# A two-layer transformer kernel: who copies the down weights of lanes 1 and 2 in the second mixture of experts

## The reference, cut to what matters

```python
N_EXPERTS_2 = 64; TOP_K_2 = 8; D_EXPERT = 256
...
    _, eidx = lax.top_k(jnp.where(emask, sel, -jnp.inf), TOP_K_2)
...
    def block_ffn(args):
        xb, e = args
        return (jax.nn.silu(xb @ w_gate[e]) * (xb @ w_up[e])) @ w_down[e]

    yb = lax.map(block_ffn, (xin, blk_e)).reshape(NB * MOE_BLOCK, D)
    y_assign = yb[dest] * sw[:, None].astype(yb.dtype)
    routed = jax.ops.segment_sum(y_assign, stok, num_segments=T)
```

## Time and profile before

| | before |
|---|---|
| runs | 3305.33, 3311.96 and 3310.26 us, median 3310.26 us |
| the profiled execution, its own time | 3302.2 us |
| its span | 3299.9 us |
| mean granted clock of TensorE | 0.952 |
| PE busy in the span | 2963.0 us, 90% |
| DVE busy | 1822.8 us, 55% |
| ACT busy | 1202.7 us, 36% |
| POOL busy | 824.5 us, 25% |

### The profile page before, as it was taken

One profiled execution on the slowest core, in us unless ns is written; L12 is line 12 of the kernel. 1 busy time (PEld: TensorE's weight loads), 2 busy tenths in 40 slices (PEclk: granted clock), 3 DMA queues, 4 the chain that ended last, 5 costly groups with the idle time before them and its releaser, 6 DMA issues. The chain is left out here.

```text
span 3299.9 us, 53016 instructions
## 1 busy us (share of the span) xinstructions
PE 2963.0 (90%) x17159; PEld 1407.0 (43%) x17160; DVE 1822.8 (55%) x2799; ACT 1202.7 (36%) x1768; POOL 824.5 (25%) x918
## 2 busy tenths in 40 slices
PE   8999989996999999498959999898889999999992
PEld 4444445553666445232326777344423322222230
DVE  3221234445777312444435777334478887888885
ACT  2222133333545100111113333021157766666774
POOL 1100000000000000144541000000058766767772
PEclk9999999997999999699978999898989999999996
DMA  6221021114122220589952000213179999999996
GB/s 242 85 107 44 0 90 51 51 50 101 52 63 67 71 72 32 221 355 417 416 216 90 26 25 29 89 49 109 67 293 317 340 377 379 316 356 350 342 303 198
DMA packets 188557, 565.56 MB, mean 171 GB/s; under 512 B 25468, under 2 KB 103904, under 8 KB 151296
## 3 DMA queue, kind: packets, MB, share of 16 engines
q1 hardware_dynamic: 146576, 425.10, 34.0%
q0 software_dynamic: 36912, 126.39, 13.2%
q10 hardware_dynamic: 4968, 12.74, 1.0%
HBM read 463.30 MB, written 100.86 MB: 171 GB/s over the span
## 5 line engine op out<-in xcount | busy, mean ns | idle before, releaser
L1561 POOL COPY moe_idx<-moe_slot_idx 128x4 int32<-128x4 int32 x4 | 0.6, 188 | 1804.3 <-DVE moe_slot_idx L1739 1804.3
L1466 POOL DMA_INDIRECT moe_xb<-token_rows,moe_idx x408 | 421.5, 1033 | 108.9 <-issue 95.0
L2135 DVE COPY h<-w_gu 128x1024 f32 (+1 forms) x342 | 266.2, 779 | 235.6 <-PE gu_ps L2003 153.7
L2029 PE MATMUL y_ps<-w_dn,hid_t 128*32 (+1 forms) x768 | 347.1, 595 | 11.4 <-ACT second L2062 7.6
L2034 PE MATMUL y_ps<-h,hid_t 128*32 128x512 f32 (+1 forms) x768 | 347.2, 595 | 0.0
L362 PE MATMUL front<-second,wcol 128*128 128x512 f32 x768 | 330.4, 592 | 4.9 <-ACTq L68 2.5
L2054 ACT ACTIVATE second<-w_gu 128x2048 f32 x146 | 271.3, 1906 | 72.8 <-issue 38.0
L1998 PE MATMUL gu_ps<-w_gu,more 128*32 x576 | 258.6, 603 | 27.3 <-DVE more L2124 15.2
L1998 PE MATMUL gu_ps<-w_gu,scores_mask 128*32 x576 | 256.7, 599 | 14.7 <-DVE h L2135 11.1
L2034 PE MATMUL y_ps<-second,hid_t 128*32 128x512 f32 x1152 | 261.8, 596 | 0.0
L2003 PE MATMUL gu_ps<-second,more 128*32 128x512 f32 x576 | 258.7, 603 | 0.0
(11 more groups left out here) (494 smaller groups left out, 6143.6 us busy)
## 6 DMA issues: line engine op xcount, KB each, us to landing
w_gu<-in_w_gate_dram SPq DMA_DIRECT2D x96, 1024.0 KB, 11.6
w_gu<-in_w_up_dram SPq DMA_DIRECT2D x96, 1024.0 KB, 14.1
w_dn<-in_w_down_dram SPq DMA_DIRECT2D x96, 1024.0 KB, 15.1
wcol<-in_w_in_dram SPq DMA_DIRECT2D x12, 1024.0 KB, 5.1
qk_by_head<-stage SPq DMA_DIRECT2D x32, 384.0 KB, 4.4
qk<-qk_by_head SPq DMA_DIRECT2D x16, 768.0 KB
expert_rows<-h ACTq DMA_DIRECT2D x24, 512.0 KB, 2.7
w_gu<-in_w_in_dram SPq DMA_DIRECT2D x20, 512.0 KB, 4.2
```

What stands on the lines that cost most here:

```text
L1466: g.indirect_dma_start(G.xb[:, slot, a, :], None, pieces, bass.IndirectOffsetOnAxis(ap=G.idx[:, slot, a:a + 1], axis=0)).then_inc(G.xb_in[ ...
L1561: g.tensor_copy(G.idx[:, b, :], G.slot_idx[:, b, :]).then_inc(idx_ready, 1)
L2029: nc.tensor.matmul(y_ps[0:SIZE, cs], hid_t[:, c, 0:SIZE], w_dn[:, bass.ds(ws, 1), c, cs].rearrange("p o n -> p (o n)"), start=c == 0, stop ...
L2135: d.tensor_copy(st_gu[a][:, :, cs, :], w_gu[:, bass.ds(ws, 1), :, cs, :].rearrange("p o g c n -> p (o g) c n")).then_inc(g_staged, 1)
```

## The change

ACT's `stage_down` copies the down weights of lanes 1 and 2; it reads two expert numbers and waits for the higher one's weights. DVE's `stage_down` copies lane 3 alone and reads one number. The semaphore counts follow: one DVE copy and two ACT copies for each block. In the first mixture DVE still copies its one lane. Nothing else differs.

```diff
@@ def finish(i) on PE
                 pe.wait_ge(d_ready, e + 1)
-                pe.wait_ge(d_staged, i * N_DVE)
+                pe.wait_ge(d_staged, i)
                 if ON_ACT:
-                    pe.wait_ge(act_d_staged, i)
+                    pe.wait_ge(act_d_staged, 2 * i)
@@ ACT
             def stage_down(b):
-                e = a.value_load(G.blk_e[0:1, 1, bass.ds(b, 1)], min_val=0, max_val=E - 1)
-                a.wait_ge(d_ready, e + 1)
+                es = [a.value_load(G.blk_e[0:1, k, bass.ds(b, 1)], min_val=0, max_val=E - 1) for k in (1, 2)]
+                a.wait_ge(d_ready, es[-1] + 1)
                 a.wait_ge(y_ready, b + 1)
-                s.activation(st_dn[1].rearrange("p c n -> p (c n)"),
-                             w_dn[:, bass.ds(e % W, 1)].rearrange("p o c n -> p (o c n)"),
-                             ACT.Copy).then_inc(act_d_staged, 1)
+                for k, e in zip((1, 2), es):
+                    s.activation(st_dn[k].rearrange("p c n -> p (c n)"),
+                                 w_dn[:, bass.ds(e % W, 1)].rearrange("p o c n -> p (o c n)"),
+                                 ACT.Copy).then_inc(act_d_staged, 1)
@@ DVE
             def stage_down(b):
-                es = experts_of(b)
-                v.wait_ge(d_ready, es[-1] + 1)
+                e = v.value_load(G.blk_e[0:1, L - 1, bass.ds(b, 1)], min_val=0, max_val=E - 1)
+                v.wait_ge(d_ready, e + 1)
                 v.wait_ge(y_ready, b + 1)
-                for a, e in zip(on_dve, es):
+                for a in (L - 1,):
                     d.tensor_copy(st_dn[a].rearrange("p c n -> p (c n)"),
                                   w_dn[:, bass.ds(e % W, 1)].rearrange("p o c n -> p (o c n)")).then_inc(d_staged, 1)
```

More of the change, by code:

```diff
@@ L1979, in _ @@
                 pool.wait_ge(g_staged, n * (PIECES * N_DVE) + PIECES * N_DVE)
-                pool.wait_ge(d_staged, n * N_DVE)
+                pool.wait_ge(d_staged, n)
                 pool.wait_ge(act_g_staged, n * 2 + 2)
-                pool.wait_ge(act_d_staged, n)
+                pool.wait_ge(act_d_staged, n * 2)
                 pool.sem_inc(rows_summed, 1)
```

## The result

The changed kernel takes 3425.71 us (median of 3 runs, 3424.72 to 3433.66) against 3310.26. The ratio is 1.0359, with a 95% interval of 1.0337 to 1.0382: slower, by 115 us. The forecast was 3385 us; the range ended at 3425, so the time lies just above it. The profiled execution has a span of 3422.3 us.

What follows compares the result with a forecast made beforehand. PE bounds undisturbed blocks at 10.94 us; the ACT-PE loop, 10.41, becomes 12.53 with copy (1.82) and load (0.3). Blocks +73.7, build-up +1, last block +2.7, slow loads +3: about +80, so 3385 us; range 3345 to 3425.

Steps and rivals of the forecast that it cites:

- the loop: ACT's down copy, PE's products, ACT's take_y, next copy: 10.41 us a block, under PE's 10.94; 12.53 after the change.
- The second load: ACT's added register load between take_y and the first down copy: 0.3 us a block, bounds 0 to 0.72.
- a few of them: +3: Register loads on ACT's loop taking over a microsecond instead of 0.28: 3 us in the sum.
- every block at the loop's length: All 69 blocks put at 12.53 us, since today's drawn-out blocks lie mostly below that.
- 73.7 + 1: 69 blocks at 12.53 us instead of 790.9 in all: +73.7; the second block's growth while the loop builds up: +1.
- The clock: Rival: PE's longer idle gap lowers its clock, +110 us more if every block pays, 3495 us; 10%.
- a fall in a few blocks only: PE's clock falling in some blocks only was said to stay within the forecast's range.
- 3358 to 3422 by the same base: The forecast's own range, from about +56 to +112 us with loops of 12.23 to 12.95 us a block.
- DVE relief: DVE's dropped copy, 1.288 us a block, priced at 0; the rival that it pays said 3290 us; 3%.
- So I add nothing for them: Today's drawn-out blocks: their gathers' lateness disappears under the longer loop, so no extra time for them.
- ACT's own work as the bound: Rival: ACT's step without idle, 11.68 us a block, sets the pace instead of the loop; some 3335 us; 5%.
- nothing changes: Rival: long blocks have room for the copy and short ones are few; 3310 us; 4%.

Runs made afterwards that it cites:

- e3: Changed kernel, but ACT reads the two expert numbers for its down copies early, right after issuing the gate and up copies: 3395.53 us, ratio 1.026.
- e7: Changed kernel, with the scatter of each block but the last replaced by a transfer of 8 elements: 3383.03 us, ratio 1.0233.
- e4: Changed kernel, with ACT's loads for the down copies and the four loads of the share copies read early: 3297.81 us, ratio 0.9974.
- e1: Changed kernel, but DVE still copies lane 2's down weights too, to a place it then overwrites: 3437.68 us, ratio 1.039.
- e9: Changed kernel, but the scatter writes its rows without adding, so token sums are not formed: 3447.95 us, ratio 1.0421.
- e2: Kernel before, without DVE's copy of lane 2 and nobody making it, so old data is used: 3301.56 us against 3307.31, ratio 0.998.

## Why the prediction was right or wrong

**What bounds the kernel, and the loop: right.** The loop's first terms, from the copy's end to the next copy, were 0.38 + 7.12 + 1.01 before; after they are 0.36, 7.17 and, with the second load, 1.32. The extra copy was put at 1.82 and measures 1.82. The second load was put at 0.3 and e3 measures 0.31. The forecast of 12.53 us stands against 12.56 in an ordinary block and 12.58 on the mean of e7. Removing the loop's sequencer-bound part (e4) removes the loss; restoring DVE's work (e1) does not.

**The step that failed is this term of the sum:** "Register loads that take over a microsecond instead of 0.28 now lie on the loop, a few of them: +3", together with putting "every block at the loop's length". I took the number of slow loads from the row of one line, where the kernel before had 4 loads of over a microsecond, and assumed that it would stay. It did not stay. The longer loop moved the share copies' loads, which had run mostly just after the scatter's start or long after it, to 2 to 4.5 us after it, and there 28 of 188 were slow.

In the profiled executions the 71 blocks grew by 117.7 us. Of this, 79.9 stay without the scatter (893.1 against 813.2), where I had 73.7 + 1 for the blocks; the loop itself was 5 us low. The other 37.8 us go with the scatter, where I had 3. They are slow loads and the falls of the clock behind them. The forecast's 80 us and these 35 more make 115, as the medians moved. That is in part chance, since the sum was built on the profiled execution, and the profiled executions lie 122 us apart.

How the 38 us divide can be estimated from the profiles. The excess is what ACT's 288 share loads took above their median, summed. The time at 1.2 GHz counts from the fourth block on; half of it is lost, since products that come 0.43 us apart come 0.85 apart there. The last column takes both off, as if all of it lay on the loop.

| kernel | 71 blocks, us | loads over 0.5 us | excess, us | at 1.2 GHz, us | blocks less both, us |
|---|---|---|---|---|---|
| changed | 930.9 | 28 | 21.5 | 37.5 | 890.6 |
| e1 | 951.7 | 45 | 31.5 | 61.4 | 889.5 |
| e9 | 958.8 | 57 | 41.6 | 51.2 | 891.6 |
| e7 | 893.1 | 0 | 0.7 | 3.4 | 890.7 |
| e3 | 900.1 | 19 | 16.6 | 27.3 | 869.9 |

The four kernels with the same ACT program come out within 2.1 us of each other, from times that are 66 us apart. So, by this estimate, some 21 of the 38 us are the loads and 17 the clock, e1's extra 21 us are the same two things, and e3 is lower by 0.29 us a block, its early load. e7 also takes DMA work away (a share of 0.74 against 0.91 between 2440 and 3200 us). That by itself does not make blocks short: e9's share is 0.77 against 0.87 between 2400 and 3400 us, and its blocks are longer.

**The clock.** The rival said that a single gap of about 1.5 us would leave the clock alone, and it does: from the fourth block on PE has 50 single gaps of 1.3 to 2.0 us in the changed kernel, and at none does the granted clock fall. Its ten falls all come at gaps of 2.04 to 3.04 us. Of the 16 gaps of over 2 us, 14 come within 12 us behind a slow load of ACT's. In e1 three of 17 falls come at gaps of 1.95 to 1.99. I allowed "a fall in a few blocks only" in the range, but priced it at nothing in the sum; by the table it is 17 us.

**The bounds.** "3358 to 3422 by the same base" is not by one base: 3302 + 56 is the one, 3310 + 112 the other. By the base of the forecast, 3305, the terms give 3361 to 3417. The measured 3425.71 lies outside either.

**DVE relief:** put at 0, worth 6 us (e2). "So I add nothing for them" about the long blocks of before was right in kind, though the gathers are hardly less late: DVE's wait for them is 35.8 us in the form that had 42.9. What is gone is PE's wait behind it, 11.1 us in its largest item before; behind DVE's copies PE now waits 1.3 us in all.

```profile
DVE more L2125 <- DMA moe_xb<-token_rows,moe_idx: 35.8, 26, 2.8
...
PE gu_ps L1998 <- DVE more L2136: 1.3, 2, 0.7
```

**Rivals.** ACT's own work as the bound (3335) fell: 12.56 us a block, and e4 runs the same copies at 11.33 us a block on the mean. That nothing changes fell as well.

The Trainium skill ("Perfetto Trace Analysis", Optimizing Scalar/DVE Operations) says that offloading some work to Scalar may make sense if DVE is saturated. DVE was the busier of the two, but busy 84% and not on the loop, and here the advice does not pay: the relief alone is worth 6 us, the move costs 115.

The rule of the Trainium skill on the queue of 8 ("Advanced Engine Details and Errata", Engine Queue Depths) would have hidden the second load. The 1.32 us between `take_y` and the copy decide against it at this place, while e4 shows the sequencer running ahead where the engine has microseconds of work queued: its four share copies come out of the queue in 0.82 us.

**The base.** I added 3 us to the profiled execution's sum for the difference to the median. The median moved by 115 us and the profiled spans by 122. The profiled execution of before lay 8 us under its median, that of the changed kernel 1 us, and this makes the 7 us.

## What to carry to other kernels

Ask of an engine not how busy it is but how much slack the loop has that runs through it: here ACT was 68% busy and had 0.53 us. A late wait elsewhere in the trace (a copy that came 0.73 us late) can lay the loop bare and give every one of its terms before the change is made. If an engine's step is a string of register loads and tiny copies, try reading the registers early, under a long instruction; here that made room for 1.8 us more work a block at no cost (e4). And a longer loop shifts the engines against each other: look not only at how much is added, but at what comes to lie next to what.

## What the runs showed that I had not expected

A register load of 0.28 us can take up to 1.5 to 1.7 us, on ACT, and it is tied to the scatter of 128 rows of 4 KB: with it the longest is 1.545 us, with it not adding 1.682, without it 0.298. What in the scatter does it is open. In e4, where the loads come while the gate and up copies run and only 1 of the 288 starts 2 to 4.5 us after the scatter's start, the longest of the share copies' loads is 0.353 us, scatter and all:

```profile
L2070 ACTq TENSOR_LOAD <-moe_blk_e x292: 272/275/353, 2396.5 to 3221.9; - x146
```

So where a load lies against the scatter matters, and not only how many there are. And the same edit, one copy more, cost three different sums: 1.82 us for the copy, 0.31 for reading its expert's number, and about 0.5 us a block (38 us over 71) for where it pushed the other loads. Of the first two the loop's slack of 0.53 us took up a part.
